# Sharing drains between two keys' searches and narrowing the pair search in a hybrid encoder layer

## The chip, the cores and the metric

One core of one Trainium2 chip runs the whole layer as one program, written by hand for each engine: TensorE (PE) multiplies, VectorE (DVE) does elementwise work and searches, ScalarE (ACT) activations, GpSimd (POOL) issues gathers, SyncE (SP) issues the other DMAs. The metric is the device time in microseconds of one execution, the median of the runs shown.

## The reference

The layer mixes 512 tokens of width 1024 (a spatial gating group and a retention group, one output projection, a LayerNorm), and then each token is sent to experts by product keys. Only the second half matters here, cut to its core:

```python
scores = jnp.einsum('bshpd,hpnd->bshpn', q, sub_keys)     # 8 heads, 2 keys, 128 scores each
top_s, top_i = lax.top_k(scores, 16)
cand_s = top_s[..., 0, :, None] + top_s[..., 1, None, :]  # 16 x 16 pairs
cand_i = top_i[..., 0, :, None] * 128 + top_i[..., 1, None, :]
best_s, best_pos = lax.top_k(cand_s, 16)                  # after a reshape to 256
expert_idx = jnp.take_along_axis(cand_i, best_pos, axis=-1)
gates = softmax(best_s)
act = gelu(einsum('td,ted->te', x, u_tab[expert_idx]))    # per token: 8 x 16 rows of u
out = einsum('te,ted->td', gates * act, v_tab[expert_idx])
```

The result is `layer_norm(alpha * h + out)`.

## The kernel before

The 512 tokens are 4 tiles of 128. The experts of tiles 0 and 1 are **gathered**: for each of the 16 units (a tile and a head) DVE finds 16 experts per token, POOL gathers the 16 rows of u and the 16 rows of v (each gather 128 rows of 4 KB, one for every token), DVE takes the dot product of each u row with the token (`product_row`, L1195) and adds each weighted v row to a sum (`add_row`, L1219). Tiles 2 and 3 are **dense**: PE multiplies them with all 16384 experts, whose u and v tables stream in as pairs of blocks of 1 MB, and a gate matrix made of one-hot products keeps what was chosen.

DVE's program is one loop over rows n = 0 to 287. Row n takes the product of u row n and adds v row n - 32. Ahead of a row come its choices (`chosen_before`): a gathered unit is chosen at rows 2, 18, 34, 50 and 66 (units 2 to 6), at rows 85, 90, 96, 102 and 108 (units 7 to 11), and at 174, 178, 194 and 210 (units 12 to 15); units 0 and 1 come before the loop. The 16 dense units are chosen at rows 24, 26, ... 54, and after each four of them one batch is looked up. Gathers run ahead of DVE in a ring of 6 u rows (POOL waits `s_dot`) and a like ring of v rows (`s_vadd`).

Three places tie DVE to PE. At row 84 (`ROUND_ROW`) the **gate round** begins: 32 groups in which DVE and ACT make one-hot matrices (`gate_rows`, L1244; ACT "half", L686 and L688), PE multiplies them (L1631) and DVE weights the activations (`dense_weights`). PE gets there when it has finished 32 activation jobs of the dense tiles (L1389). After it PE runs expert jobs (L1460), and from the 34th on it needs one **team** of one-hots for each two experts (L1644 on PE, `team_rows_of`, L1263 on DVE). DVE makes the first team at row 115. In rows 145 to 206 DVE also multiplies the second half's activations (`gated_gelu`, L1297), which PE needs later.

One choice of a gathered unit is `choose(..., False)`, `positions` and `look_up`. `choose` runs `top16` for one key and then for the other (MAX8, FIND_INDEX8, MATCH_REPLACE8, MAX8, FIND_INDEX8 over 128 scores), adds the two sorted lists to 256 sums and runs `top16` on those. `positions` splits a position into a row and a column, `look_up` compares these with a table (512 bf16 elements), multiplies by the key numbers, halves the sum four times, and a last operation makes 128 * key1 + key2. `fence` is DVE's drain instruction; it stands wherever an operation reads what the one before has written. A dense unit is chosen over 112 sums instead of 256.

Of the kernel before, what the change touches and what calls it, by code (L numbers as in the profile page):

```python
# [5 lines left out]
P = 128  # L6
# [5 lines left out]
PH, TOPK, NK = 8, 16, 128  # L12
# [5 lines left out]
GATHERED = 2  # L18
# [68 lines left out]

BATCH = 4
WIDE = 4
PAIRS = WIDE * TOPK + (TOPK - WIDE) * WIDE  # L90


HEAD_ORDER = list(range(TILE0, PH)) + list(range(TILE0))
# [4 lines left out]
NEG = -3.0e38  # L98
# [192 lines left out]
def layer(nc, x, w_in, sgu_ln_w, sgu_ln_b, sgu_w_s, sgu_b, decay_fwd, decay_bwd, gn_w, w_out, ln1_w, ln1_b,  # L291
# [6 lines left out]
    ALU, ACT = mybir.AluOpType, mybir.ActivationFunctionType  # L298
    AX = mybir.AxisListType
# [7 lines left out]
    with ctx:  # L307
        def sb(name, shape, dt=f32):
            return ctx.enter_context(nc.sbuf_tensor(name, shape, dt))
# [48 lines left out]
        S4 = S.rearrange("p (t q n) -> p t q n", t=NT, q=2 * PH)  # L358
# [27 lines left out]
        ohi = sb("ohi", [P, 2, 2, PIECES, HALF, 4], f16)  # L386
        grid = sb("grid", [P, NK, 4], f16)
        table = sb("table", [P, TOPK, TOPK], bf16)
        work = sb("work", [P, 512])
        lookg = work[:, 0:256].bitcast(bf16)  # L390
        ohi16 = ohi[:].rearrange("p b q c n t -> p b (q c n t)").rearrange(
# [10 lines left out]
        iota = sb("iota", [P, NK])  # L402
# [7 lines left out]
        top = sb("top", [P, 2, TOPK])  # L410
        topi = sb("topi", [P, BATCH + 1, 2, TOPK], u32)
        pos = sb("pos", [P, BATCH + 1, TOPK], u32)
        posab = sb("posab", [P, BATCH, 2, TOPK], u32)
        topb = sb("topb", [P, BATCH, 2, TOPK, 4], bf16)
        posb = sb("posb", [P, BATCH, 2, TOPK], bf16)
        pick = sb("pick", [P, 2, TOPK])
        best = sb("best", [P, GUNITS, TOPK])
        idx = sb("idx", [P, GUNITS, TOPK], i32)
        negmax = sb("negmax", [P, GUNITS])
# [47 lines left out]
        s_idx = sem("indices_ready")  # L467
# [404 lines left out]
        def _(dve):  # L872
# [200 lines left out]
            def top16(src, values, index, spare):  # L1073

                V.max(values[:, 0:8], src)
                fence()
                V.max_index(index[:, 0:8], values[:, 0:8], src)  # L1077
                V.match_replace(spare, values[:, 0:8], src, NEG)  # L1078
                fence()
                V.max(values[:, 8:16], spare)  # L1080
                fence()
                V.max_index(index[:, 8:16], values[:, 8:16], spare)

            def choose(scores, values, slot, pruned):

                cand = work[:, 0:PAIRS if pruned else 256]
                spare = work[:, 256:512]
                for p in range(2):
                    top16(scores[:, p, :], top[:, p, :], topi[:, slot, p, :], spare[:, p * NK:(p + 1) * NK])
                fence()  # L1090
                for a0, a1, width in ((0, WIDE, TOPK), (WIDE, TOPK, WIDE)) if pruned else ((0, TOPK, TOPK),):
                    c = a0 * TOPK
                    a = top[:, 0, a0:a1].unsqueeze(2).broadcast_to([P, a1 - a0, width])
                    bb = top[:, 1, 0:width].unsqueeze(1).broadcast_to([P, a1 - a0, width])
                    V.tensor_tensor(cand[:, c:c + (a1 - a0) * width].rearrange("p (a b) -> p a b", b=width), a, bb,
                                    ALU.add)
                fence()
                top16(cand, values, pos[:, slot, :], spare[:, 0:cand.shape[-1]])
                fence()

            def positions():

                p = posb[:, 0, :, :]
                V.tensor_scalar(posab[:, 0, 0, :], pos[:, BATCH, :], 4, None, ALU.logical_shift_right)
                V.tensor_scalar(posab[:, 0, 1, :], pos[:, BATCH, :], 15, None, ALU.bitwise_and)
                fence()
                V.tensor_copy(p, posab[:, 0])

            def pruned_positions():

# [14 lines left out]
            def look_up(slots, mem, chosen):  # L1125

                n = 2 * (slots.stop - slots.start)
                tb = topb[:, 0:n // 2].rearrange("p s q k r -> p (s q k) r")
                pb = posb[:, 0:n // 2].rearrange("p s q k -> p (s q) k")
                V.tensor_copy(tb, topi[:, slots].rearrange("p s q k -> p (s q k)").unsqueeze(2).broadcast_to(  # L1130
                    [P, n * TOPK, 4]))
                fence()
                e = mem[:, 0:n * 256].rearrange("p (q a k) -> p q a k", q=n, a=TOPK)
                e4 = mem[:, 0:n * 256].rearrange("p (q k r) -> p q k r", q=n * TOPK, r=4)
                V.tensor_tensor(e, pb.unsqueeze(2).broadcast_to([P, n, TOPK, TOPK]),
                                table[:].unsqueeze(1).broadcast_to([P, n, TOPK, TOPK]), ALU.is_equal)
                fence()
                V.tensor_tensor(e4, e4, tb.unsqueeze(2).broadcast_to([P, n * TOPK, 4, 4]), ALU.mult)
                for width in (8, 4, 2):
                    fence()  # L1140
                    V.tensor_tensor(e[:, :, 0:width, :], e[:, :, 0:width, :], e[:, :, width:2 * width, :], ALU.add)
                fence()
                for s in range(n // 2):
                    V.tensor_tensor(chosen(s), e[:, 2 * s:2 * s + 2, 0, :], e[:, 2 * s:2 * s + 2, 1, :], ALU.add)
                fence()

            def choose_gathered(u):
                t, h = divmod(u, PH)
                if t == 0 and h < TILE0:
                    dve.wait_ge(s_sc0, h + 1)  # L1150
                elif t == 0:
                    dve.wait_ge(s_sc, 2 * (h - TILE0) + 2)
                else:
                    dve.wait_ge(s_sc, 2 * PH)
                choose(S4[:, t, 2 * h:2 * h + 2, :], best[:, u, :], BATCH, False)
                positions()
                look_up(slice(BATCH, BATCH + 1), lookg, lambda s: pick[:])
                V.scalar_tensor_tensor(idx[:, u, :], pick[:, 0, :], float(NK), pick[:, 1, :],
                                       ALU.mult, ALU.add).then_inc(s_idx, 1)
                V.tensor_scalar(negmax[:, u:u + 1], best[:, u, 0:1], -1.0, None, ALU.mult).then_inc(s_best, 1)  # L1160

            def choose_dense(n):
                i, a = divmod(n, 2)
                h = HEAD_ORDER[i]
                dve.wait_ge(s_sc, 2 * i + 2)
                choose(S4[:, GATHERED + a, 2 * h:2 * h + 2, :], gated[:, a * PH + h, :], n % BATCH, True)
                fence().then_inc(s_chosen, 1)
                if n % BATCH == BATCH - 1:
                    pruned_positions()
                    look_up(slice(0, BATCH), lookd,  # L1170
                            lambda s: sel[:, s % 2, :, HEAD_ORDER[(n - BATCH + 1 + s) // 2], :])
# [148 lines left out]

            V.tensor_copy(grid[:], iota[:].unsqueeze(2).broadcast_to([P, NK, 4]))
            V.tensor_copy(table[:], iota[:, 0:TOPK].unsqueeze(2).broadcast_to([P, TOPK, TOPK]))
            dve.wait_ge(s_ln, 32)
            residual(0, 0)
            fence()
# [380 lines left out]
```

## Time and profile before

| | |
|---|---|
| median of 3 runs | 1464.63 us (1461.72 to 1469.0) |
| span of the profiled execution | 1462.8 us |
| PE busy | 1367.2 us (93%) |
| DVE busy | 1143.9 us (78%) |
| POOL busy | 662.1 us (45%) |
| ACT busy | 397.7 us (27%) |
| DMA | 444.28 MB, mean 304 GB/s |

A busy share is a mean over stages with different limits. The stages are told apart by the table of stretches, which gives each engine's busy time, the clock granted to PE, the mean busy share of the 16 DMA engines and the rate. What limits a stage is then read from its waits: an engine that never idles in the stage, and for which another one waits at its end, sets it.

### The profile page before, as it was taken

Reading aid. Unit: us, or ns where it says so; the run is one execution under the profiler, and the core shown is the slowest. Engines: PE = TensorE matmul, PEld = TensorE weight load, DVE = VectorE, ACT = ScalarE, POOL = GpSimd, SP = SyncE. Lnnn points to the kernel's source line nnn. Section 1 sums busy time; section 2 is a strip of 40 time slices with the busy share of each in tenths; the row PEclk is TensorE's granted clock in tenths of the full one; section 3 lists DMA queues with packets and bytes.
Section 4 is the critical chain, followed back from the end, with each engine's and each line's share of the span. In section 5 each row is a group of like instructions: output and inputs, shape, how many; then the busy total and the mean of one; then the engine's idle time right before and its main releaser. Section 6 shows DMA issues by size and latency. Waiting matters only on the chain.

```text
span 1462.8 us, 18813 instructions
## 1 busy us (share of the span) xinstructions
PE 1367.2 (93%) x6494; PEld 959.0 (66%) x6494; DVE 1143.9 (78%) x2495; ACT 397.7 (27%) x815; POOL 662.1 (45%) x548
## 2 busy tenths in 40 slices
PE   8999989799999999979999599999999999999953
PEld 6787755488888888867544255578888854444421
DVE  4837266678888888789889998878999887766787
ACT  4224000512120101259410064666651010000020
POOL 2334111353332345620245566545445665766673
PEclk9999999999999999999999799999999999999986
DMA  6411234576878789982499999999899999999996
GB/s 237 151 59 58 93 138 144 187 252 223 311 266 315 288 309 414 414 332 85 169 395 398 391 382 414 407 362 393 332 364 353 415 413 414 414 413 414 412 360 258
DMA packets 118430, 444.28 MB, mean 304 GB/s; under 512 B 11712, under 2 KB 24512, under 8 KB 101952
## 3 DMA queue, kind: packets, MB, share of 16 engines
q0 software_dynamic: 73728, 268.47, 48.2%
q1 hardware_dynamic: 44032, 173.56, 30.8%
q8 instruction: 52, 0.85, 0.2%
q10 hardware_dynamic: 576, 1.05, 0.2%
q14 instruction: 42, 0.34, 0.1%
HBM read 440.94 MB, written 2.10 MB: 303 GB/s over the span
## 4 chain that ended last, share of the span: by engine, by line
DVE 32%; PE 29%; DMA 16%; POOL 6%; issue 6%; DVEq 5%; ACT 4%; ACTq 1%; SPq 0%
DMA big<-in_peer_v_dram,idx 10%; DVE y L1219 8%; PE ps L1460 7%; DVE big L1195 7%; PE ps L1406 7%; PE ps L1389 6%; DMA big<-in_peer_u_dram,idx 6%; POOL big L636 4%; POOL big L620 2%; PE ps L1553 2%; PE ps L1644 2%; DVE work L1078 2%; ACT wr L686 2%; DVE topi L1077 1%; DVE top L1080 1%
## 5 line engine op out<-in xcount | busy, mean ns | idle before, releaser
L620 POOL DMA_INDIRECT big<-in_peer_u_dram,idx x256 | 311.8, 1218 | 538.1 <-DVE dots L1195 431.6
L1195 DVE CUSTOM_DVE_ANT_0 big<-big,xh 128x1024 f32<-128x1024 f32 x256 | 311.7, 1224 | 64.7 <-DMA big<-in_peer_u_dram,idx 42.6
L1219 DVE SCALAR_TENSOR_TENSOR y<-big,wgt,y 128x1024 f32<-128x1024 f32 x245 | 314.0, 1282 | 45.0 <-DMA big<-in_peer_v_dram,idx 41.3
L636 POOL DMA_INDIRECT big<-in_peer_v_dram,idx x256 | 289.4, 1130 | 103.7 <-issue 67.7
L1460 PE MATMUL ps<-big,pool_mem 128*128 128x512 f32 x512 | 224.3, 594 | 0.0
L1389 PE MATMUL ps<-xT,big 128*128 128x256 f32 x960 | 211.1, 380 | 0.0
L1389 PEld LDWEIGHTS ps<-xT,big 128*128 128x128 f32 x960 | 182.2, 191 | 23.9
L1460 PEld LDWEIGHTS ps<-big,pool_mem 128*128 128x128 f32 x512 | 97.0, 191 | 118.4 <-issue 118.4
L1460 PE MATMUL ps<-y,pool_mem 128*128 128x512 f32 x256 | 114.8, 600 | 0.0
L1460 PE MATMUL ps<-xT,pool_mem 128*128 128x512 f32 x256 | 113.5, 594 | 0.0
L1389 PE MATMUL ps<-xT 128*128 128x256 f32 x480 | 106.4, 380 | 0.0
L1389 PE MATMUL ps<-xT,y 128*128 128x256 f32 x480 | 106.4, 380 | 0.0
L1389 PE MATMUL ps<-xT,pool_mem 128*128 128x256 f32 (+1 forms) x512 | 102.4, 360 | 2.7 <-ACTq L778 2.4
L1389 PEld LDWEIGHTS ps<-xT 128*128 128x128 f32 x480 | 91.1, 191 | 12.0
L1389 PEld LDWEIGHTS ps<-xT,y 128*128 128x128 f32 x480 | 91.1, 191 | 11.9
L1389 PEld LDWEIGHTS ps<-xT,pool_mem 128*128 128x128 f32 x512 | 88.1, 195 | 13.2 <-issue 3.4
L1460 PEld LDWEIGHTS ps<-y,pool_mem 128*128 128x128 f32 x256 | 48.9, 193 | 59.3 <-issue 59.0
L496 POOL TENSOR_TENSOR weight_parts<-big,weight_parts 128x1024 fp32r<-128x1024 f32 x20 | 49.0, 2470 | 85.0 <-ACT weight_parts L652 84.9
L1460 PEld LDWEIGHTS ps<-xT,pool_mem 128*128 128x128 f32 x256 | 48.5, 191 | 59.2 <-issue 59.2
L694 ACT ACTIVATE sel<-iota,gated 128x128 f16<-128x128 f32 x256 | 83.7, 553 | 0.1
L1406 PE MATMUL ps<-weight_parts,x_hi 128*128 128x512 f32 x320 | 82.9, 404 | 0.8 <-ACT weight_parts L652 0.8
L652 ACT ACTIVATE pool_mem<-ps 128x512 f32<-128x512 f32 (+2 forms) x52 | 28.5, 548 | 181.3 <-PE ps L1389 86.9
(253 smaller groups left out, 1586.9 us busy)
## 6 DMA issues: line engine op xcount, KB each, us to landing
big<-u_pairs_dram SPq DMA_DIRECT2D x32, 1024.0 KB, 8.0
big<-v_pairs_dram SPq DMA_DIRECT2D x32, 1024.0 KB, 8.1
y<-u_pairs_dram SPq DMA_DIRECT2D x16, 1024.0 KB, 7.9
xT<-u_pairs_dram SPq DMA_DIRECT2D x16, 1024.0 KB, 7.8
y<-v_pairs_dram SPq DMA_DIRECT2D x16, 1024.0 KB, 7.9
xT<-v_pairs_dram SPq DMA_DIRECT2D x16, 1024.0 KB, 8.0
big<-in_w_in_dram SPq DMA_DIRECT2D x24, 512.0 KB, 5.7
pool_mem<-in_peer_w_q_dram SPq DMA_DIRECT2D x12, 1024.0 KB, 7.6
```

Source lines behind the costliest of these rows:

```text
L496: return engine.tensor_tensor(w_lo(g)[:, ks, :], w_full(g)[:, ks, :], w_hi(g)[:, ks, :].bitcast(f32), ALU.subtract)
L620: nc.gpsimd.indirect_dma_start(urow[n % RING], None, peer_u2, bass.IndirectOffsetOnAxis(ap=idx[:, u, e:e + 1], axis=0)).then_inc(s_u[n % R ...
L636: nc.gpsimd.indirect_dma_start(vrow[place], None, peer_v2, bass.IndirectOffsetOnAxis(ap=idx[:, u, e:e + 1], axis=0)).then_inc(s_v[place], 16)
L686: A.activation(four[:, :, t], iota[:], ACT.Abs, bias=minus_key[:, c:c + 1])
L694: A.activation(ohl[:, t // 4, :, t % 4], iota[:], ACT.Abs, bias=minus_key[:, c:c + 1])
L1078: V.match_replace(spare, values[:, 0:8], src, NEG)
L1195: V.tensor_tensor_reduce(out=urow[n % RING], in0=urow[n % RING], in1=xh[:, u // PH * D:(u // PH + 1) * D], scale=1.0, scalar=0.0, op0=ALU. ...
L1219: V.scalar_tensor_tensor(acc_rows[t], vrow[place], wgt[:, u % 2, e:e + 1], acc_rows[t], ALU.mult, ALU.add).then_inc(s_vadd, 1)
L1389: last = T.matmul(dst, lhs(i), rhs(i), start=(i == 0), stop=(i == n - 1))
L1406: last = T.matmul(dst, *((a, b_) if x_left else (b_, a)), start=(n == 0 and k == 0), stop=(n == 2 and k == KC - 1))
L1460: last = T.matmul(acc[a][:, half * 512:(half + 1) * 512], X[:, i, a * P:(a + 1) * P], rows_v[:, half * 512:(half + 1) * 512], start=False, ...
L1553: T.matmul(bank, mixT[:, k, t * P:(t + 1) * P], w[:, k, :], start=(k == 0), stop=False)
```

## The change

Both keys' searches run side by side in `choose`: two MAX8, one drain, two pairs of FIND_INDEX8 and MATCH_REPLACE8, one drain, two MAX8, one drain; the last FIND_INDEX8 of each key stands beside the sums. The closing drain of `choose` is gone. This holds for the gathered and the dense units. The gathered units search 136 sums (row 0 with 16 columns, rows 1 to 15 with 8 each) in place of 256. `find_gathered` takes the place of `positions` and of `look_up` for them: the key numbers are scaled by 128 and 1 as they are copied, a position of the new layout is turned into row and column, and one TENSOR_REDUCE over the 32 products of each choice (both keys) writes the index. `negmax` is made earlier in the unit. The cut diff:

```diff
+DENSE_PAIRS = ((0, WIDE, TOPK), (WIDE, TOPK, WIDE))
+GATHER_PAIRS = ((0, 1, TOPK), (1, TOPK, TOPK // 2))
+        strides = sb("strides", [P, 2])
-        pick = sb("pick", [P, 2, TOPK])
...
@@ -1081,30 +1082,58 @@
                 fence()
                 V.max_index(index[:, 8:16], values[:, 8:16], spare)
 
-            def choose(scores, values, slot, pruned):
-
-                cand = work[:, 0:PAIRS if pruned else 256]
+            def choose(scores, values, slot, layout):
+
+                width = sum((a1 - a0) * w for a0, a1, w in layout)
+                cand = work[:, 0:width]
                 spare = work[:, 256:512]
+                keep = [spare[:, p * NK:(p + 1) * NK] for p in range(2)]
                 for p in range(2):
-                    top16(scores[:, p, :], top[:, p, :], topi[:, slot, p, :], spare[:, p * NK:(p + 1) * NK])
-                fence()
-                for a0, a1, width in ((0, WIDE, TOPK), (WIDE, TOPK, WIDE)) if pruned else ((0, TOPK, TOPK),):
-                    c = a0 * TOPK
-                    a = top[:, 0, a0:a1].unsqueeze(2).broadcast_to([P, a1 - a0, width])
-                    bb = top[:, 1, 0:width].unsqueeze(1).broadcast_to([P, a1 - a0, width])
-                    V.tensor_tensor(cand[:, c:c + (a1 - a0) * width].rearrange("p (a b) -> p a b", b=width), a, bb,
-                                    ALU.add)
-                fence()
-                top16(cand, values, pos[:, slot, :], spare[:, 0:cand.shape[-1]])
-                fence()
-
-            def positions():
-
-                p = posb[:, 0, :, :]
-                V.tensor_scalar(posab[:, 0, 0, :], pos[:, BATCH, :], 4, None, ALU.logical_shift_right)
-                V.tensor_scalar(posab[:, 0, 1, :], pos[:, BATCH, :], 15, None, ALU.bitwise_and)
-                fence()
-                V.tensor_copy(p, posab[:, 0])
+                    V.max(top[:, p, 0:8], scores[:, p, :])
+                fence()
+                for p in range(2):
+                    V.max_index(topi[:, slot, p, 0:8], top[:, p, 0:8], scores[:, p, :])
+                    V.match_replace(keep[p], top[:, p, 0:8], scores[:, p, :], NEG)
+                fence()
+                for p in range(2):
+                    V.max(top[:, p, 8:16], keep[p])
+                fence()
+                c = 0
+                for a0, a1, w in layout:
+                    a = top[:, 0, a0:a1].unsqueeze(2).broadcast_to([P, a1 - a0, w])
+                    bb = top[:, 1, 0:w].unsqueeze(1).broadcast_to([P, a1 - a0, w])
+                    V.tensor_tensor(cand[:, c:c + (a1 - a0) * w].rearrange("p (a b) -> p a b", b=w), a, bb, ALU.add)
+                    c += (a1 - a0) * w
+                for p in range(2):
+                    V.max_index(topi[:, slot, p, 8:16], top[:, p, 8:16], keep[p])
+                fence()
+                top16(cand, values, pos[:, slot, :], spare[:, 0:width])
+
+            def find_gathered(u):
+
+                numbers = topb[:, 0].rearrange("p q k r -> p (q k) r")
+                V.tensor_tensor(topb[:, 0], topi[:, BATCH].unsqueeze(3).broadcast_to([P, 2, TOPK, 4]),
+                                strides[:].unsqueeze(2).unsqueeze(3).broadcast_to([P, 2, TOPK, 4]), ALU.mult)
+                V.tensor_scalar(negmax[:, u:u + 1], best[:, u, 0:1], -1.0, None, ALU.mult).then_inc(s_best, 1)
+                fence()
+                p = pos[:, BATCH, :]
+                V.tensor_scalar(posab[:, 0, 0, :], p, 3, None, ALU.logical_shift_right)
+                V.tensor_scalar(posab[:, 0, 1, :], p, 7, None, ALU.bitwise_and)
+                V.scalar_tensor_tensor(posab[:, 1, 0, :], p, 16.0, p, ALU.is_lt, ALU.mult)
+                fence()
+                V.tensor_scalar(posb[:, 0, 0, :], posab[:, 0, 0, :], 1.0, 1.0, ALU.max, ALU.subtract)
+                V.tensor_tensor(posb[:, 0, 1, :], posab[:, 0, 1, :], posab[:, 1, 0, :], ALU.max)
+                fence()
+                e = lookg.rearrange("p (q a k) -> p q a k", q=2, a=TOPK)
+                e4 = lookg.rearrange("p (q k r) -> p q k r", q=2 * TOPK, r=4)
+                V.tensor_tensor(e, posb[:, 0].unsqueeze(2).broadcast_to([P, 2, TOPK, TOPK]), 
+                                table[:].unsqueeze(1).broadcast_to([P, 2, TOPK, TOPK]), ALU.is_equal)
+                fence()
+                V.tensor_tensor(e4, e4, numbers.unsqueeze(2).broadcast_to([P, 2 * TOPK, 4, 4]), ALU.mult)
+                fence()
+                with nc.allow_low_precision(reason="one nonzero whole number per key"):
+                    V.tensor_reduce(idx[:, u, :], lookg.rearrange("p (c k) -> p k c", k=TOPK), AX.X, ALU.add
+                                    ).then_inc(s_idx, 1)
 
             def pruned_positions():
 
@@ -1152,18 +1181,14 @@
                     dve.wait_ge(s_sc, 2 * (h - TILE0) + 2)
                 else:
                     dve.wait_ge(s_sc, 2 * PH)
-                choose(S4[:, t, 2 * h:2 * h + 2, :], best[:, u, :], BATCH, False)
-                positions()
-                look_up(slice(BATCH, BATCH + 1), lookg, lambda s: pick[:])
-                V.scalar_tensor_tensor(idx[:, u, :], pick[:, 0, :], float(NK), pick[:, 1, :],
-                                       ALU.mult, ALU.add).then_inc(s_idx, 1)
-                V.tensor_scalar(negmax[:, u:u + 1], best[:, u, 0:1], -1.0, None, ALU.mult).then_inc(s_best, 1)
+                choose(S4[:, t, 2 * h:2 * h + 2, :], best[:, u, :], BATCH, GATHER_PAIRS)
+                find_gathered(u)
 
             def choose_dense(n):
                 i, a = divmod(n, 2)
                 h = HEAD_ORDER[i]
                 dve.wait_ge(s_sc, 2 * i + 2)
-                choose(S4[:, GATHERED + a, 2 * h:2 * h + 2, :], gated[:, a * PH + h, :], n % BATCH, True)
+                choose(S4[:, GATHERED + a, 2 * h:2 * h + 2, :], gated[:, a * PH + h, :], n % BATCH, DENSE_PAIRS)
                 fence().then_inc(s_chosen, 1)
                 if n % BATCH == BATCH - 1:
                     pruned_positions()
@@ -1320,6 +1345,7 @@
 
             V.tensor_copy(grid[:], iota[:].unsqueeze(2).broadcast_to([P, NK, 4]))
             V.tensor_copy(table[:], iota[:, 0:TOPK].unsqueeze(2).broadcast_to([P, TOPK, TOPK]))
+            V.tensor_scalar(strides[:], iota[:, 0:2], 1.0 - NK, float(NK), ALU.mult, ALU.add)
             dve.wait_ge(s_ln, 32)
             residual(0, 0)
             fence()
```

## Rows read from the trace of the kernel before

**Rows 1.** Stretches: busy us of PE, PEld, DVE, ACT, POOL; clock, DMA share, GB/s.
```profile
300.00:540.00 240.00, 237.89 (x1211) 210.75 (x1210) 205.13 (x704) 38.29 (x66) 84.42 (x74) 1.00 0.79 280
540.00:640.00 100.00, 92.80 (x449) 82.05 (x447) 80.69 (x134) 19.51 (x36) 63.17 (x57) 0.99 1.02 411
708.00:730.00 22.00, 22.00 (x52) 9.83 (x53) 20.03 (x52) 6.73 (x10) 9.37 (x8) 1.00 0.73 254
730.00:839.00 109.00, 91.57 (x219) 40.42 (x218) 98.80 (x235) 3.79 (x10) 55.79 (x54) 0.94 1.00 395
839.00:950.00 111.00, 111.00 (x667) 57.12 (x666) 97.00 (x135) 64.67 (x150) 67.27 (x57) 0.98 1.01 400
950.00:1130.00 180.00, 179.46 (x1283) 153.74 (x1282) 156.79 (x281) 90.11 (x203) 90.94 (x79) 1.00 0.94 360
1130.00:1440.00 310.00, 288.88 (x771) 147.35 (x770) 232.41 (x355) 34.53 (x62) 202.68 (x166) 0.97 1.01 406
```

**Rows 2.** Timeline of PE: start, us, line, out<-in, count, [idle before it <-releaser].
```profile
625.73 7.07 PE L1389 MATMUL ps<-xT 128*128 128x256 f32 x32
640.29 1.15 PE L1631 MATMUL ps<-ohi,wr 128*128 128x64 f16 x16 [7.49 <-DVEq L1244]
...
817.83 3.60 PE L1460 MATMUL ps<-y,pool_mem 128*128 128x512 f32 x8
838.86 0.69 PE L1644 MATMUL ps<-ohi,wr 128*128 128x32 f16 x16 [17.43 <-DVEq L1263]
...
1390.19 7.03 PE L1460 MATMUL ps<-xT,pool_mem 128*128 128x512 f32 x16
```

**Rows 3.** Timeline of DVE: the choice of unit 9 and the row after it.
```profile
757.99 0.29 DVE L1075 MAX8 top<-pool_mem 128x8 f32<-128x128 f32 x1
758.36 0.09 DVE L1077 MATCH_VALUE_LOAD topi<-top,pool_mem 128x8 f32 x1
758.43 0.28 DVE L1077 FIND_INDEX8 topi<-top,pool_mem 128x8 uint32<-128x128 f32 x1
758.64 0.07 DVE L1078 MATCH_VALUE_LOAD work<-top,pool_mem 128x8 f32 x1
...
767.63 1.22 DVE L1195 CUSTOM_DVE_ANT_0 big<-big,xh 128x1024 f32<-128x1024 f32 x1
```

**Rows 4.** Timeline of DVE: a dense unit's choice, the row after, the gate round's start.
```profile
333.31 0.29 DVE L1075 MAX8 top<-pool_mem 128x8 f32<-128x128 f32 x1
...
339.18 1.23 DVE L1195 CUSTOM_DVE_ANT_0 big<-big,xh 128x1024 f32<-128x1024 f32 x1 [0.20 <-issue]
...
636.97 0.29 DVE L1270 CAST pieces<-work 128x256 f16<-128x256 f32 x1
```

**Rows 5.** Groups of DVE by shape: busy us, mean ns of one, idle before.
```profile
L1219 DVE SCALAR_TENSOR_TENSOR y<-big,wgt,y 128x1024 f32<-128x1024 f32 x245 | 314.0, 1282 | 45.0 <-DMA big<-in_peer_v_dram,idx 41.3 <-issue 0.7
L1195 DVE CUSTOM_DVE_ANT_0 big<-big,xh 128x1024 f32<-128x1024 f32 x256 | 311.7, 1224 | 64.7 <-DMA big<-in_peer_u_dram,idx 42.6 <-issue 5.6
L1080 DVE MAX8 top<-work 128x8 f32<-128x128 f32 x64 | 18.8, 294 | 4.7
L1075 DVE MAX8 best<-work 128x8 f32<-128x256 f32 x16 | 6.8, 428 | 1.2
L1141 DVE TENSOR_TENSOR work<-work 128x256 bf16<-128x256 bf16 x16 | 4.7, 292 | 1.2
L1182 DVE TENSOR_REDUCE dsum<-gated 128x16 f32<-128x256 f32 x1 | 0.4, 420 | 0.1
```

**Rows 6.** Timeline of ACT where the gate round begins.
```profile
635.07 0.63 ACT L688 ACTIVATE wr<-wr 128x512 f16<-128x512 f16 x1
...
644.31 1.47 ACT L686 ACTIVATE wr<-iota,gated 128x128 f16<-128x128 f32 x4 [0.66 <-PE ps L1631]
```

**Rows 7.** Gathers issued in 708 to 840 us: count, median us from issue to landing.
```profile
big<-in_peer_u_dram,idx POOLq DMA_INDIRECT x31, 10.4
```

**Rows 8.** Timeline of DVE: unit 13's choice begins.
```profile
1105.72 0.29 DVE L1075 MAX8 top<-pool_mem 128x8 f32<-128x128 f32 x1
```

More of the change, by code:

```diff
@@ L89 @@
 WIDE = 4
-PAIRS = WIDE * TOPK + (TOPK - WIDE) * WIDE
+DENSE_PAIRS = ((0, WIDE, TOPK), (WIDE, TOPK, WIDE))
+GATHER_PAIRS = ((0, 1, TOPK), (1, TOPK, TOPK // 2))
 HEAD_ORDER = list(range(TILE0, PH)) + list(range(TILE0))
```

## The prediction, made before the changed kernel ran

> **What bounds the kernel now.** I read the stretches first [rows 1], then what PE waits for [rows 2], then DVE's own timeline around those two waits [rows 3, 4]. The stretches show four stages. From 300 to 540 us the DMA engines are busy 0.79 of the time and DVE works through the choices. From 540 to 640 us they are full (1.02, 411 GB/s). From 708 to 839 us DVE is busy 118.8 of 131 us, the rest being little gaps around its instructions, and the DMA share climbs to 1.00 at 395 GB/s. From 839 to 1130 us the share is between 0.94 and 1.01 with 360 to 400 GB/s, and from 1130 us to the end of the gathers it is full again at 406 GB/s.
>
> PE, busy 93% of the span, is held by DVE at two places only [rows 2]. At the gate round it is ready at 632.8 us and starts at 640.29, 7.49 us later, since DVE begins the round's first operation at 636.97 [rows 4]. At the first team it is ready at 821.4 us and starts at 838.86, 17.43 us later, since DVE comes late to row 115. From there PE runs without a gap to the end of the experts at 1397.2 us [rows 2], while the last gathers follow at the DMA's full rate. So whatever brings the team of 838.86 us forward brings everything behind it forward, as long as the gathers keep their distance. That is the quantity to work out.
>
> **One gathered unit.** Unit 9's choice takes from 757.99 to 767.63 us, 9.64 us [rows 3]. What a drain costs is in the same rows: behind MAX8 (757.99 + 0.29 = 758.28) the next operation starts at 758.36, 0.08 later; behind FIND_INDEX8 (758.43 + 0.28 = 758.71), with no drain, the next starts at 758.64, 0.07 earlier. A drain so costs 0.15 us of order.
> Drains: 20 before (7 in and behind the two keys, 1 behind the sums, 3 in the pair search, 1 behind it, 1 between positions and copy, 7 in the look-up), 12 after (7 in `choose`, 5 in `find_gathered`). 8 x 0.15 = 1.20 us.
> Size: MAX8 takes 428 ns over 256 and 294 over 128, 1.05 ns for one element [rows 5]. The pair search has five passes (two MAX8, two FIND_INDEX8, one MATCH_REPLACE8) that shrink by 120 elements: 5 x 0.126 = 0.63 us. The sums, one operation of 256 before, become 16 and 120 in two, whose lengths fall by the same 0.126 while a second start of 0.09 is added: 0.04 us. FIND_INDEX8 and MATCH_REPLACE8 are given MAX8's slope, since both scan the same elements.
> Finding the expert: gone are three halvings (292 ns the first [rows 5], near 0.2 the smaller), the last addition, a cast and the multiply-add, also under 0.2. Less the 0.08 by which each overlaps the next that is 0.78 us. Added are 0.07 for key numbers that are multiplied in place of copied, three small operations at 0.09, 0.28 together, and the reduction. That last form is not in the trace with this layout: TENSOR_REDUCE over 256 elements takes 420 ns [rows 5], over 512 I take 420 + 256 x 1.05 = 0.69 us, 0.61 without its overlap. Net 0.18 us more.
> Sum: 1.20 + 0.63 + 0.04 - 0.18 = 1.7 us less for each gathered unit. The bounds: if the reduction packed its bf16 input as the halvings do (256 elements in 292 ns) it took 0.43, and the sum is 2.0; if reading every 16th element cost it three times its length, 1.4 us more, the sum is 0.3 (and the whole gain, by the steps below, about 5 us: 1460). I take the middle, because the only reduction of the trace is an ordinary one at MAX8's rate.
> The Trainium skill has a rule against this step: VectorE: DVE Perf Modes, Rules for kernel authors, says of `tensor_reduce` "Expect 1× — it's the slowest DVE op", which it would have restructured. The one-element rate agrees with the 420 ns of [rows 5] (by that page's perf mode table four halvings may run at two elements a cycle); it is in the sum already.
>
> **One dense unit.** Choice and drains take 339.18 - 333.31 = 5.87 us [rows 4]. Its sizes stay. The keys and sums have 8 drains before and 4 after, and behind the choice two drains become one: 5 x 0.15 = 0.75; as two drains in a row overlap, I take 0.7 us. 16 units: 11 us.
>
> **Up to the gate round.** Units 0 and 1 and what comes before about 325 us lie in front of a wait of DVE for PE's scores and give nothing. Behind that DVE has 16 dense units and units 4 and 5 before 540 us, 11 + 2 x 1.7 = 14.6 us. In this stage the DMA has room (0.79, 280 GB/s [rows 1]). The full stretch of 540 to 640 us starts that much earlier and ends that much earlier, since the gathers in it are the same and the dense loads take their share by PE's time. DVE then stands at the gate round at about 637 - 15 = 622 us and PE, whose activations run without a gap, is there at 632.8 as before [rows 2]: DVE's wait is gone and PE and ACT are late next. ACT finishes the round's first one-hots at 635.07 + 0.63 = 635.7 [rows 6], since the last activation goes before them; the second ones need about 2.1 more, 637.8. It then needs PE's first group, which follows at about 636.3, so its fourth group starts at 639.7 where before it starts at 644.31 [rows 6]. From there ACT, PE and DVE share a step of about 2.1 us. The round ends 4.6 us earlier; the other 10 us of DVE's lead are lost in waiting for PE.
>
> **From the gate round to the team.** DVE chooses units 7 to 11 before row 115, all on the path to the team: 5 x 1.7 = 8.5 us. PE's own work there shifts by 4.6 only, so its wait of 17.43 shrinks to about 9 and stays a wait: the whole 8.5 counts. The cost of it is DMA. 730 to 839 us carries 395 x 109 = 43.1 MB [rows 1]; with four choices in it the stretch becomes 102.2 us and would want 421 GB/s, against 411 in the full stretch before the round. At 411 it takes 104.9 us, 2.7 us more. Against this the rings hold 6 rows, 6 x (1.224 + 1.282) = 15.0 us of DVE's work [rows 5], and a gather lands after 10.4 us [rows 7], so nearly 5 us of lateness cost nothing at first. I take 1.0 us.
>
> **Behind the team.** PE is shifted by 4.6 + 7.5 = 12.1 us. DVE is paced by PE in the teams up to about 1030 us and then by itself until 1130 us, where units 12 and 13 are chosen (the latter at 1105.72 [rows 8]) and the DMA moves 360 GB/s [rows 1], room enough for rows that come earlier. 2 x 1.7 = 3.4 us; of this I leave 0.5 to the DMA. Units 14 and 15 lie in the full stretch, where DVE has time: nothing. One small operation for the strides lies at about 200 us in a wait for PE.
> Sum: 4.6 + 7.5 + 2.9 = 15.0 us. The profiled span becomes 1462.8 - 15.0 = 1447.8. The median of the runs lies 1.8 above the span, so **1449.6 us**. Its own range, with the unit's sum between 1.2 and 2.0 us (7 units that count: -3.5 to +2.1) and the DMA's part between 0 and 4 us, is 1445 to 1456.
>
> **Rivals.**
> *The DMA takes the gain back* (chance 0.17). For it: the share is 1.00 from 730 us on, and 395 GB/s is what the stretch moves. If it could move no more, only the choice of unit 7 (before 730 us) helps, 1.7, with 4.6 of the round and perhaps 2 of units 12 and 13: 8.3 us, 1456. Against it: the gathers land in 10.4 us, before they are wanted, and 406 to 411 GB/s are moved elsewhere.
> *Shared drains save nothing* (0.04), the change not doing what it says. If the order between operations were the same with and without a drain, a gathered unit would gain 0.5 us and a dense one nothing. DVE's lead at the round is 1.0 us, the five units give 2.5, the later two 1.0: 4.5 us, 1460. The 0.08 behind and 0.07 before in [rows 3] speak against it.
> The Trainium skill states this rule: VectorE: DVE Perf Modes, The DRAIN you can't avoid, says that a chain of operations takes the same time with a semaphore after each or only at the end, so that one minimises their count. The trace does not agree for the explicit drain: 0.15 us each.
> *Slower* (0.04): the reduction reads one bf16 of every 32 bytes. Were each such read to cost as much as nine elements, it took 512 x 9 x 1.05 = 4.8 us in place of 0.69, and the unit would be 2.4 us longer than before. Most of the round's gain, 4 us, stays (the dense units give 11, units 4 and 5 take 4.8), seven units cost 16.8: 1477 us. It decides at 1.7 + 0.66 = 2.4 us over my estimate, a reduction of 3.1 us; above 4.1 us the kernel is slower by over 0.5%. Against it: nothing in the trace reads so slowly.
> *The lead before the round is smaller* (0.07), because the full DMA stretch does not start earlier: then the round shifts by 0 to 4 us, 1452.
> *More than forecast* (0.08): PE runs at 1.2 of 2.4 GHz for a while behind its long waits (clock 0.94 in 730 to 839 us [rows 1]) and loses less behind shorter ones, and the DMA hides all: 1443.
>
> **Chances.** The forecast has 0.60. No measurement of this kernel tells less than about 0.5% (7.3 us, 1457.3 us) from no change. Faster by more than that: 0.60 + 0.07 + 0.08 + two thirds of the DMA rival, 0.85, less something for terms that I have not seen, 0.82. Within it 0.13, slower 0.05. The range reaches to the DMA rival and its spread above and to the full gain below: 1442 to 1460.
>
> **What would show it.** PE's wait before the gate round's first group should fall from 7.49 to under 3 us and be one for ACT; DVE should wait at the round. PE's wait before the first team should be 8 to 10 us. A gathered choice should take 7.9 us and a dense one 5.2. The reduction should read near 690 ns. DVE should show little or no waiting for gathers before 839 us. If PE's wait at the team has shrunk by the full 8.5 us and the end has not moved, the gathers are the bound and the sum's last steps are wrong; if the choices have not shrunk, its first.

## The result

The changed kernel takes 1451.91 us, median of 4 runs (1449.52 to 1453.66), against 1463.85 us of the kernel before beside it: a ratio of 0.9914, 95% interval 0.9895 to 0.9933, so 12 us less with an interval of about 10 to 15. Forecast were 1449.6 us and a range of 1442 to 1460. The profiled execution has a span of 1451.7 us.

The stretches of after, the same as in [rows 1] (busy us of PE, PEld, DVE, ACT, POOL; clock, DMA share, GB/s):

```profile
300.00:540.00 240.00, 237.92 (x1211) 210.33 (x1210) 207.81 (x716) 37.71 (x65) 93.21 (x83) 1.00 0.82 292
540.00:640.00 100.00, 97.53 (x486) 86.19 (x485) 71.22 (x126) 19.83 (x37) 55.61 (x48) 1.00 1.02 413
708.00:730.00 22.00, 22.00 (x53) 9.80 (x52) 20.30 (x56) 4.71 (x8) 11.51 (x11) 1.00 0.81 298
730.00:839.00 109.00, 98.83 (x256) 44.02 (x255) 100.97 (x235) 7.95 (x20) 58.67 (x57) 0.95 1.02 410
839.00:950.00 111.00, 111.00 (x671) 57.03 (x670) 95.04 (x134) 64.69 (x150) 67.63 (x58) 1.00 1.02 407
950.00:1130.00 180.00, 179.47 (x1275) 156.66 (x1274) 159.03 (x282) 89.49 (x198) 94.33 (x82) 1.00 0.94 365
```

Ahead of the gate round DVE is less busy (71.2 us of 100, 80.7 before) at the same DMA rate. It waits 7.0 us for PE there, and 17.6 us for gathers where it waited 13.7. From 730 to 839 us the DMA engines move 410 GB/s where they moved 395. The two waits of PE that answer to [rows 2], in its timeline:

```profile
628.26 7.07 PE L1415 MATMUL ps<-xT 128*128 128x256 f32 x32
635.16 0.65 PE L1657 MATMUL ps<-ohi,wr 128*128 128x64 f16 x8
638.29 0.67 PE L1657 MATMUL ps<-ohi,wr 128*128 128x64 f16 x8 [2.48 <-ACT wr L689]
...
829.47 0.69 PE L1670 MATMUL ps<-ohi,wr 128*128 128x32 f16 x16 [10.17 <-DVEq L1288]
830.00 0.69 PE L1670 MATMUL ps<-ohi,sel 128*128 128x32 f16 x16
830.53 5.67 PE L1486 MATMUL ps<-y,pool_mem 128*128 128x512 f32 x8
836.03 3.60 PE L1486 MATMUL ps<-big,pool_mem 128*128 128x512 f32 x8
```

At the gate round PE no longer waits 7.49 us for DVE: it does the first half of a group and waits 2.48 us for ACT's one-hots. At the first team it waits 10.17 us in place of 17.43. DVE, in its own timeline, is ready for the round early and stands still there (as [rows 4] has it late):

```profile
627.35 0.29 DVE L1295 CAST pieces<-work 128x256 f16<-128x256 f32 x1
...
638.99 0.69 DVE L1307 SCALAR_TENSOR_TENSOR pool_mem<-ps,pool_mem 128x512 f32<-128x512 f32 x1 [7.00 <-PE ps L1657]
...
705.81 1.23 DVE L1220 CUSTOM_DVE_ANT_0 big<-big,xh 128x1024 f32<-128x1024 f32 x1 [0.18 <-issue]
```

A gathered choice of after, unit 9, and the row after it (DVE's timeline, most rows left out; [rows 3] for before):

```profile
753.13 0.49 DVE L1092 MAX8 top<-pool_mem 128x8 f32<-128x128 f32 x2
753.69 0.09 DVE L1095 MATCH_VALUE_LOAD topi<-top,pool_mem 128x8 f32 x1
...
760.34 1.08 DVE L1135 TENSOR_REDUCE idx<-work 128x16 int32<-128x512 bf16 x1
761.34 1.21 DVE L1220 CUSTOM_DVE_ANT_0 big<-big,xh 128x1024 f32<-128x1024 f32 x1
```

The two MAX8 take 0.49 us together, side by side with no drain. And the groups by shape (busy us, mean ns of one, idle before) that answer to [rows 5]:

```profile
L1135 DVE TENSOR_REDUCE idx<-work 128x16 int32<-128x512 bf16 x16 | 17.2, 1077 | 1.2
L1099 DVE MAX8 top<-work 128x8 f32<-128x128 f32 x64 | 15.6, 285 | 2.4
L1076 DVE MAX8 best<-work 128x8 f32<-128x136 f32 x16 | 4.8, 303 | 1.2
L1078 DVE FIND_INDEX8 pos<-best,work 128x8 uint32<-128x136 f32 x16 | 4.7, 294 | 0.0
```

Read off between the first MAX8 and the row behind the choice, a gathered unit takes 8.21 us in most places where it took 9.65 in most, a dense one 5.15 where it took 5.88: 1.44 and 0.73 us less. Single units are up to 0.4 us longer in either kernel. Over 16 and 16 units that is 34.7 us of DVE's time, for 12 us of the kernel's.

### The profile page after: what moved, and what is told of

It reads as the page before. It is cut to its first block, busy times and chain, and to the rows that moved or that the text cites. A ratio compares the mean times of both kernels' runs of the same rounds, so it can differ in the third digit from the quotient of the medians.

```text
span 1451.7 us, 18590 instructions
## 1 busy us (share of the span) xinstructions
PE 1370.0 (94%) x6494; PEld 959.2 (66%) x6494; DVE 1124.7 (77%) x2480; ACT 397.5 (27%) x815; POOL 662.3 (46%) x548
## 4 chain that ended last, share of the span: by engine, by line
PE 56%; DVE 16%; DMA 13%; POOL 4%; ACT 4%; issue 3%; DVEq 2%; ACTq 1%; SPq 0%
PE ps L1415 30%; DMA big<-in_peer_v_dram,idx 8%; PE ps L1486 7%; PE ps L1432 7%; DVE y L1244 5%; DMA big<-in_peer_u_dram,idx 4%; DVE big L1220 3%; POOL big L637 3%; PE ps L1670 2%; PE ps L1579 2%; POOL big L621 2%; ACT wr L687 2%; ACT wr L689 1%; PE ps L1600 1%; PE ps L1573 1%
## 5 line engine op out<-in xcount | busy, mean ns | idle before, releaser
L637 POOL DMA_INDIRECT big<-in_peer_v_dram,idx x256 | 289.3, 1130 | 108.7 <-issue 67.7
L1415 PEld LDWEIGHTS ps<-xT 128*128 128x128 f32 x480 | 90.9, 190 | 12.2
```

What stands on the lines that cost most here:

```text
L637: nc.gpsimd.indirect_dma_start(vrow[place], None, peer_v2, bass.IndirectOffsetOnAxis(ap=idx[:, u, e:e + 1], axis=0)).then_inc(s_v[place], 16)
L1415: last = T.matmul(dst, lhs(i), rhs(i), start=(i == 0), stop=(i == n - 1))
```

## The experiments

Two theories run through them. Mine, from the prediction: only what shortens PE's two waits for DVE counts (and something behind the first team). The rival: DVE's time counts alike wherever it is saved, 12 of 34.7 us, 0.34 for each.

### The change in halves by place

New code for one set of units, old code for the rest, both sets of functions in one program:

```diff
-                choose(S4[:, t, 2 * h:2 * h + 2, :], best[:, u, :], BATCH, GATHER_PAIRS)
-                find_gathered(u)
+                if u >= 7:        # the second kernel: u < 7, and the new code for all dense units
+                    choose(S4[:, t, 2 * h:2 * h + 2, :], best[:, u, :], BATCH, GATHER_PAIRS)
+                    find_gathered(u)
+                    return
+                choose_one_key_at_a_time(S4[:, t, 2 * h:2 * h + 2, :], best[:, u, :], BATCH, False)
+                positions()
...
```

> The new code for the gathered units 7 to 15 alone; units 0 to 6 and all dense units are chosen as before. Nine units are shortened, by the 1.44 us that the trace of after shows for one, 13.0 us of DVE's order in all. My theory (only PE's two waits for DVE count): the wait at the gate round stays 7.5 us, the wait at the first team falls from 17.4 to about 10.3 us, units 12 and 13 give 1.7 to 2.9 more: 1463.85 - 9.5 = 1454.4 us. Rival (DVE time counts everywhere alike, at the share that after shows, 11.9 us for 34.7 us of order saved, 0.34): 4.5 us, 1459.4.

Measured: 1456.88 us against 1464.31, ratio 0.9945 (0.9926 to 0.9965), 7.4 us less; the 9.5 that I expected are still inside the interval. PE's timeline:

```profile
639.02 1.16 PE L1696 MATMUL ps<-ohi,wr 128*128 128x64 f16 x16 [7.47 <-DVEq L1308]
...
830.49 0.69 PE L1709 MATMUL ps<-ohi,wr 128*128 128x32 f16 x16 [10.35 <-DVEq L1327]
```

> The complement: new code for units 0 to 6 and all 16 dense units, old code from unit 7 on. 7 x 1.44 + 16 x 0.73 = 21.8 us of DVE's order are saved, all ahead of the gate round. My theory: PE's wait there falls from 7.5 to about 2.5 us and is one for ACT, DVE waits some 7 us at the round, the wait at the first team stays near 17.4 us, gain 4.7 us: 1459.2 us. Rival (alike everywhere): 0.34 x 21.8 = 7.4 us, 1456.4.

Measured: 1459.79 us against 1464.31, ratio 0.9967 (0.9956 to 0.9979), 4.5 us less:

```profile
634.76 0.66 PE L1696 MATMUL ps<-ohi,wr 128*128 128x64 f16 x8 [2.47 <-ACT wr L691]
...
833.12 0.69 PE L1709 MATMUL ps<-ohi,wr 128*128 128x32 f16 x16 [17.30 <-DVEq L1327]
```

Each half moves its own wait and leaves the other at before's length. 13.0 us of DVE's time saved behind the round's start bring 7.4 us; 21.8 us saved ahead of it bring 4.5. The rival had them the other way round (4.5 and 7.4); both its numbers lie outside the measured intervals, and it falls.

### The change in halves by kind

> The kernel before with the two keys' searches side by side and nothing else: 256 sums, old positions and look-up. A dense unit should take 5.15 us of 5.88, a gathered one 9.05 of 9.65 (4 drains at 0.15). My theory: round 4.7, units 7 to 11 3.0, behind the team 0.8: 8.5 us, 1455.4 us. Rival that a drain costs nothing in itself (what counts is the number of operations): units as long as before, 1463.9 us.

The edit is `choose` of after with one layout of 16 x 16 for gathered units and a drain behind it. Measured: 1455.05 us against 1464.31, ratio 0.9936 (0.9916 to 0.9956), 9.3 us less. A gathered unit takes 8.97 us, a dense one 5.15; PE waits 2.47 us at the round and 13.88 at the team. So the shared drains alone carry most of the change, and a drain costs 0.17 us here ((9.65 - 8.97) / 4). The rival, units as long as before, falls.

> After with one key's search behind the other's, as before, and the closing drain of the choice; 136 sums and the one summation stay. A gathered unit should take 8.8 us, a dense one 5.88. My theory: 2 x 0.84 ahead of the round 1.7, units 7 to 11 4.2, behind the team 1.2: 7.1 us, 1456.8 us. With the run before this would sum to more than after's gain (8.5 + 7.1 against 11.9), since the round gives 4.7 us only once. Rival (effects add up): 11.9 - 8.5 = 3.4 us, 1460.4.

```diff
+                for p in range(2):
+                    top16(scores[:, p, :], top[:, p, :], topi[:, slot, p, :], spare[:, p * NK:(p + 1) * NK])
+                fence()
...
                 top16(cand, values, pos[:, slot, :], spare[:, 0:width])
+                fence()
```

Measured: 1461.24 us against 1464.31, ratio 0.9978 (0.9966 to 0.9989), 3.1 us less and not 7.1: a miss of my numbers.

```profile
638.80 1.16 PE L1648 MATMUL ps<-ohi,wr 128*128 128x64 f16 x16 [6.74 <-DVEq L1260]
...
834.39 0.69 PE L1661 MATMUL ps<-ohi,wr 128*128 128x32 f16 x16 [14.49 <-DVEq L1279]
```

A unit takes 9.07 us, 0.58 less, not 0.84: this kernel has five drains more than after, the closing one among them, and at 0.17 us each they are the 0.86 us between 8.21 and 9.07. Five units give 2.9 us at the team (17.43 to 14.49), two give 0.75 at the round. So the waits hold and the size of the unit was wrong. The gains of the two halves, 9.3 and 3.1, sum to 12.4, near the 11.9 and 13.2 of the whole change, as the rival of adding up had it. In the waits two things cancel. The round's gain is counted twice (5.02 and 0.75 us, 5.01 in after). The closing drain of a gathered unit is in neither half, which costs the halves about 0.8 us at the team (3.55 and 2.94 us, 7.26 in after).

### Where a choice stands

After's DVE stands still at the round. If that is lost time, a choice moved into it is free:

```diff
-LATER_CHOICES = {ROUND_ROW + 1: 7, ROUND_ROW + 6: 8, ...}
+LATER_CHOICES = {58: 6, 62: 7, ROUND_ROW + 6: 8, ...}
```

> After, with unit 6 chosen at row 58 and unit 7 at row 62 in place of rows 66 and 85, that is ahead of the gate round, where DVE waits 17.6 us for gathers and 7.0 us for PE. My theory (only PE's two waits for DVE count): the choice of 8.2 us leaves the path to the first team, PE's wait there falls from 10.2 to 2 us, the round stays where it is: 1451.9 - 8.2 = 1443.7 us. Rival (DVE's time counts wherever it stands, and none is saved): 1451.9. Rival (the gathers become the bound behind the round): the wait at the team shrinks and the span behind the team grows by as much.

Measured: 1441.25 us against 1464.32, ratio 0.9844 (0.9826 to 0.9862): 23 us under before and 10.7 under after.

```profile
634.65 0.66 PE L1657 MATMUL ps<-ohi,wr 128*128 128x64 f16 x8 [2.48 <-ACT wr L689]
...
817.73 0.69 PE L1670 MATMUL ps<-ohi,wr 128*128 128x32 f16 x16 [2.04 <-DVEq L1288]
818.26 0.69 PE L1670 MATMUL ps<-ohi,sel 128*128 128x32 f16 x16
818.79 3.68 PE L1486 MATMUL ps<-y,pool_mem 128*128 128x512 f32 x8
```

The round's wait is unchanged, the team's falls by 8.13 us, and not an instruction is saved. Another 2 us, which I had not expected, are in the last row: the first expert's 8 matmuls behind the wait take 3.68 us, behind after's wait of 10.17 us they take 5.67. In before they take 4.92, behind 17.43 us:

```profile
839.93 4.92 PE L1460 MATMUL ps<-y,pool_mem 128*128 128x512 f32 x8
```

> After, with units 6, 7 and 8 chosen at rows 58, 61 and 64: 16.4 us of choices leave the path to the first team, where PE waits 10.2 us, so PE's own work is the bound from the round on and DVE waits. My theory: 10.2 us less if DVE's waits ahead of the round hide both choices, 1441.7 us, and only 2.0 less than with unit 7 alone; if they hide only the first, the round comes later by up to 8 us and the time is near 1446. Rival (alike everywhere): 1451.9.

The edit is `{58: 6, 61: 7, 64: 8, ...}`. Measured: 1438.92 us against 1464.32, ratio 0.9823 (0.9805 to 0.984), the fastest version of this study: 13 us under after, and 2.3 us under the kernel with unit 7 alone, where I expected 2.0. DVE is just late at the round, and there is no wait for DVE at the team any more:

```profile
634.24 0.66 PE L1657 MATMUL ps<-ohi,wr 128*128 128x64 f16 x8 [1.55 <-DVEq L1269]
635.66 0.66 PE L1657 MATMUL ps<-ohi,wr 128*128 128x64 f16 x8 [0.76 <-ACT wr L689]
...
814.81 1.88 PE L1486 MATMUL ps<-y,pool_mem 128*128 128x512 f32 x4
816.52 0.68 PE L1670 MATMUL ps<-ohi,wr 128*128 128x32 f16 x16
```

Its stretches show PE without a gap from 730 to 839 us, so that PE's own work sets the pace there, and the DMA engines full:

```profile
708.00:730.00 22.00, 22.00 (x53) 9.80 (x52) 20.81 (x27) 2.15 (x4) 16.71 (x18) 1.00 0.98 376
730.00:839.00 109.00, 109.00 (x343) 49.93 (x343) 95.14 (x206) 19.46 (x45) 62.22 (x55) 1.00 1.02 413
839.00:950.00 111.00, 110.46 (x684) 59.59 (x684) 92.63 (x130) 61.60 (x145) 68.38 (x55) 1.00 1.02 413
```

DVE waits 6.8 us for gathers between 708 and 840 us here, and in after not at all. PE does not feel it in this version; whether the gathers would hold up a next step is not shown.

> The kernel before with the same move of units 6 and 7. There DVE is late at the round already (PE waits 7.5 us). My theory: the wait at the team falls by 9.65 to near 8 us; the wait at the round grows by what DVE's 12 us of waits for gathers before it do not hide, near 2 us: 1464.3 - 7.6 = 1456.7 us. Rival (without a lead at the round the move only shifts the loss): the wait at the round grows by 9.65 us, 1464.3.

Measured: 1462.28 us against 1464.32, ratio 0.9991 (0.9981 to 1.0001), 2 us less, which is not clear of noise.

```profile
645.62 1.16 PE L1631 MATMUL ps<-ohi,wr 128*128 128x64 f16 x16 [14.83 <-DVEq L1244]
...
834.72 0.69 PE L1644 MATMUL ps<-ohi,wr 128*128 128x32 f16 x16 [7.90 <-DVEq L1263]
```

The team's wait falls by 9.5 us and the round's grows by 7.3, where I had expected 2: DVE's waits for gathers between 540 and 640 us shrink from 13.7 us to 11.3 only. The rival (9.65 and no gain) is much nearer than I was. The same move that brings 10.7 us behind the change brings 2 us at most ahead of it. So the change also bought a lead at the round, which after itself does not use.

### The reduction

> After with nine more reductions of zeros by DVE ahead of the first norm, 512 elements to 16 and once 256: bf16 and f32 input, read with a stride of 16 elements or in one piece, written as i32 or f32. In the choices the form bf16, strided, i32 took 1.08 us, 2.0 cycles of 0.96 GHz for an element, where I took 0.69. If the stride is the cause, the forms in one piece take 0.69 and the strided f32 1.08 as well; if the bf16 input or the integer output is, the stride makes no difference. The whole is up to 9 us longer.

The edit is a loop of V.tensor_reduce over `work`, with the stride ("p (c k) -> p k c", k = 16) and without. The rows:

```profile
199.77 1.08 DVE L1356 TENSOR_REDUCE triali<-work 128x16 int32<-128x512 bf16 x1
200.93 0.69 DVE L1358 TENSOR_REDUCE triali<-work 128x16 int32<-128x512 bf16 x1
...
205.45 1.01 DVE L1356 TENSOR_REDUCE trialf<-work 128x16 f32<-128x512 f32 x1
206.53 0.69 DVE L1358 TENSOR_REDUCE trialf<-work 128x16 f32<-128x512 f32 x1
```

L1356 reads with the stride, L1358 in one piece. The 0.69 us of the forecast is right for a reduction in one piece, in all four pairs of types (bf16 or f32 in, int32 or f32 out). The stride of 16 elements adds 0.39 us to bf16 and 0.32 to f32, with either output. (One execution, with nine reductions more: 1454.43 us.)

> After with the one reduction of 1.08 us replaced by three halvings, the last addition of each key and the sum of the two keys, five operations with drains between: 0.36 + 0.30 + 0.26 + 0.26 + 0.18 = 1.36 us of order against 1.00. A gathered unit should take 8.6 us in place of 8.2, and by my theory only the five between the round and the first team count: 1.8 us, 1453.7 us, the wait at the team 12.0 us. Rival (by its rate for one element the reduction is the dearer way): a unit under 8.2 us and the time below 1451.9.

```diff
-                    V.tensor_reduce(idx[:, u, :], lookg.rearrange("p (c k) -> p k c", k=TOPK), AX.X, ALU.add
-                                    ).then_inc(s_idx, 1)
+                for width in (8, 4, 2):
+                    V.tensor_tensor(e[:, :, 0:width, :], e[:, :, 0:width, :], e[:, :, width:2 * width, :], ALU.add)
+                    fence()
+                V.tensor_tensor(pick[:], e[:, :, 0, :], e[:, :, 1, :], ALU.add)
+                fence()
+                V.tensor_tensor(idx[:, u, :], pick[:, 0, :], pick[:, 1, :], ALU.add).then_inc(s_idx, 1)
```

Measured: 1452.56 us against 1464.42, ratio 0.9911 (0.9894 to 0.9927), which after's own spread covers; but the unit takes 8.51 us and PE's wait at the team is 11.95 us (10.17 with the reduction). So the one reduction, dear as it is, is worth 0.3 us a unit and 1.8 us at the team, against the operations and drains that it replaces. The median does not resolve this.

### Behind the first team

> After with the old code for units 12 to 15 alone, which are chosen behind the first team; units 0 to 11 and the dense ones are as in after. Four units take 1.44 us more. If behind the team DVE's time up to unit 13 counts, as the prediction had it, 1.4 to 2.9 us more than after: 1453.3 to 1454.8 us, and the span from the first team to the end grows from 622.2 us by as much. If the gathers set the pace there, no change: 1451.9 us.

Measured: 1452.58 us against 1464.42, ratio 0.9921 (0.9908 to 0.9935); its profile has the team at 824.80 us and a span of 1450.4, so 625.6 us behind the team. The median is 0.7 us over after's, and 1.4 over that of after's repeat below.

> After with unit 7 ahead of the round and with the old code for units 12 to 15, which are chosen behind the first team. From the team to the end the profiles so far show 621.0, 622.2 and 622.4 us where these four units are new and 623.9, 624.6, 625.6 and 625.6 where they are old. If DVE's time behind the team counts, this one shows near 625 and a time of 1441.25 + 3 = 1444 us; if the difference is scatter, 621 to 622 and 1441.

Measured: 1445.10 us against 1464.4, ratio 0.987 (0.9851 to 0.9888); team at 817.22 us, span 1440.0, 622.8 us behind it. Against the 1441.25 us with the new code there, 3.9 us more.

> After, unchanged, once more. In the profiled execution of after PE came to the gate round at 635.3 us, in that of before at 632.8 and in those of six other variants between 630.6 and 632.7, though the code up to about 220 us differs by nothing but one small operation. If that is a scatter between executions, this profile has PE at the round near 631 to 633 us and a span near 1449; if it belongs to the kernel, 635 again. The stretch from PE's arrival to the first team should be 194.1 us again, that from the team to the end 622.2.

Measured: 1451.19 us against 1464.4, ratio 0.9904 (0.9885 to 0.9924). PE comes to the round at 633.8 us, the team starts at 828.04 and the span is 1450.3: 194.2 us between them, as in the first profile of after (194.1), and 622.3 behind.

From the team to the end ten profiles have: 621.0, 622.2, 622.3, 622.4 and 624.4 us where units 12 to 15 are chosen by the whole new code (the 624.4 is the run with the nine reductions, which I had left out of the list above), and 622.8, 623.9, 624.6, 625.6 and 625.6 where they are chosen by the old. The means are 622.5 and 624.5 us, and the two sets overlap. One row of PE's timeline is clearer. Behind its last expert PE waits for the last gathered rows of v. The rows are those of before, after, after with old code in 12 to 15, after with unit 7 early and the old code in 12 to 15, and after with unit 7 early, in this order:

```profile
1409.43 3.46 PE L1664 MATMUL ps<-big,wr 128*128 128x512 f32 x4 [12.20 <-DMA big<-in_peer_v_dram,idx]
1399.38 1.19 PE L1690 MATMUL ps<-big,wr 128*128 128x512 f32 x1 [10.95 <-DMA big<-in_peer_v_dram,idx]
1396.54 3.57 PE L1729 MATMUL ps<-big,wr 128*128 128x512 f32 x4 [12.69 <-DMA big<-in_peer_v_dram,idx]
1386.87 3.59 PE L1729 MATMUL ps<-big,wr 128*128 128x512 f32 x4 [12.54 <-DMA big<-in_peer_v_dram,idx]
1385.32 8.37 PE L1690 MATMUL ps<-big,wr 128*128 128x512 f32 x12 [10.62 <-DMA big<-in_peer_v_dram,idx]
```

In the five profiles with the new code this wait is 10.6 to 11.0 us, in the five with the old 12.2 to 12.7 us. (With units 7 and 8 early, which has the new code too but no wait at the team, it is 11.8.) The old code in units 12 to 15 alone makes it 1.7 and 1.9 us longer. So DVE's time behind the team counts through this third wait, by about 1.7 us. Which of units 12 to 15 do it no run separates.

### The waits and the medians

| kernel | wait at round | wait at team | both less than before's 24.9 | wait for the last v rows (before: 12.2) | medians less |
|---|---|---|---|---|---|
| after | 2.48 | 10.17 | 12.3 | 11.0 | 11.9 and 13.2 |
| new from unit 7 | 7.47 | 10.35 | 7.1 | 10.6 | 7.4 |
| new before the round | 2.47 | 17.30 | 5.2 | 12.5 | 4.5 |
| shared drains only | 2.47 | 13.88 | 8.6 | 11.3 | 9.3 |
| all but shared drains | 6.74 | 14.49 | 3.7 | 12.2 | 3.1 |
| before, unit 7 early | 14.83 | 7.90 | 2.2 | 12.2 | 2.0 |
| halvings | 2.47 | 11.95 | 10.5 | 11.5 | 11.9 |
| after, old in 12 to 15 | 2.48 | 10.20 | 12.2 | 12.7 | 11.8 |
| after, unit 7 early | 2.48 | 2.04 | 20.4 | 10.6 | 23.1 |
| the same, old in 12 to 15 | 2.47 | 2.04 | 20.4 | 12.5 | 19.3 |
| after, units 7 and 8 early | 1.55 + 0.76 | none | 22.6 | 11.8 | 25.4 |

Two numbers of one timeline give the gain of the first eight versions within 1.4 us, seven of them within 1 us. Two of the last three gain 2.7 and 2.8 more than their waits. Of this 1.2 us is PE's faster start behind a short wait (3.68 us for the first 8 matmuls, 4.92 in before), and 1.6 and 0.4 us are the third wait; that is all of the 2.7, and 1.2 of the 2.8 stay open. The version between them gains 1.1 us less than its waits; its profiled run, 1441.94 us, lies 3.2 us under its median.

## Why the prediction was right, and where not

**The direction and the size** were right: 15.0 us forecast, 12 and 13.2 in two comparisons. The mechanism was right as well, that PE's two waits for DVE are the currency, for all but the last of these terms:

- *A gathered unit, 1.7 us*: measured 1.44. The term that was mis-sized is the reduction, 1.08 us against 0.69. It was costed by the only reduction of the trace, which reads in one piece, and the layout was named as the unknown, but its price was left at nothing. The other terms together came out 0.13 better. The 0.15 us for a drain measures 0.17 with shared drains only, which over 8 drains is 0.16 us; MAX8 over 136 elements took 303 ns, as forecast.
- *A dense unit, 0.7 us*: 0.73.
- *The round, 4.6 us*: from PE's arrival (635.33) to DVE's first row behind it (705.81) 70.48 us, before 632.80 to 707.94, 75.14: 4.66 us. That ACT is late next was right (2.48 <-ACT). That the rest of DVE's lead is lost was right too, and the kernel with unit 7 early shows its worth.
- *Round to team, 7.5 us*: 130.92 us before (707.94 to 838.86), 123.66 after: 7.26. Two errors cancel here, by luck. The units gave 7.0 and not 8.5, and the 1.0 us kept back for the DMA was not needed: DVE did not wait for a gather in this stretch in either kernel. The DMA engines moved 410 GB/s, about as much as in the full stretch ahead of the round (413), and gathers still landed in time. The rival that the DMA takes the gain back so falls: at a share of 1.00 and 395 GB/s the engines could still move more.
- *Behind the team, 2.9 us*: 1.7 between the two profiles, 2.0 between the means of ten. The direction was right and the size about 1 us too large. The prediction took it from DVE's time before 1130 us and named no wait of PE for it; the runs show it as the wait of PE for the last rows of v, which the prediction did not have.
- *What the sum has no term for*: PE comes to the round 2.5 us later in after's profile, at 635.33 us against 632.80, through code that the change hardly touches. The three measured terms are 4.66 + 7.26 + 1.7 = 13.6 us; less 2.5 they are the 11.1 us between the two spans. Of the 2.5 us, 1.0 is lost by 128 us (the clock from 50 to 100 us is 0.93, 0.97 before), and 1.7 by PE's first output matmuls: 16 of them took 8.82 us (L1573) where the same took 7.13 in before's profile (L1547), the clock from 200 to 250 us being 0.93 and 0.97. Over the 14 profiles of this study PE comes to the round between 630.6 and 635.4 us. The four latest are those of after, its repeat, the halvings and the nine reductions, but the earliest is that of after with old code in units 12 to 15, whose code up to the round is after's. Whether after has a late start more often than before is open, and with it how much of the 2 to 3 us between 15.0 and 12 to 13 it explains.

**The rivals.** Shared drains do save time, 9.3 us by themselves. The Trainium skill (VectorE: DVE Perf Modes, "The DRAIN you can't avoid") says that a chain of operations takes the same time with a semaphore after each or only after the last; for the explicit drains of this kernel that does not hold, at 0.15 to 0.17 us for each. A slow strided reduction was real, but 1.57 times its length and not nine reads for one. The lead before the round was smaller than forecast, 8.0 us (627.35 to 635.33) and not nearly 11 (622 to 632.8), but larger than the change could use. The rival of more than forecast, that PE loses less to its clock behind a shorter wait, did not come true in after: the first 8 matmuls took 5.67 us behind 10.17 us of waiting and 4.92 behind 17.43.

## What to carry to other kernels

Count an engine's saving only at the places where the engine that sets the pace waits for it; 34.7 us saved here were worth 12, which is within 1 us what two waits in one timeline lost. Where a saving leaves an engine standing still, look for work behind the next meeting point that can be moved ahead of it: that was worth 13 us more, as much as the change itself brought, for one line. And take the price of an operation from one with its own access pattern, or measure it by itself ahead of the use.

## What was not expected of the hardware

- A reduction of 512 elements to 16 takes 0.69 us read in one piece and 1.08 us (bf16) or 1.01 us (f32) read with a stride of 16 elements.
- A drain between two operations of DVE that do not need it costs 0.15 to 0.17 us, more than half of the 0.28 us that one of these operations takes.
- PE is slower right behind a long wait, but its loss does not grow with the wait. The first 8 matmuls of 512 columns took 3.68 us behind a wait of 2.04 us, and behind longer ones 5.94 (7.90), 5.67 (10.17), 4.91 (10.35), 5.87 (11.95), 4.67 (13.88), 6.24 (14.49), 5.57 (17.30) and 4.92 (17.43). The granted clock of after is 0.61 from 829.4 to 836.0 us, a mean between the levels of 1.2 and 2.4 GHz, and 1.00 from 836 us on, where the next 8 take 3.60 us again. So a wait of 10 us cost PE 12.
